# Root per token, padded queries and head pairs, score blocks on ScalarE: one diffusion-backbone step on Trainium2

## The reference

```python
def rms_norm(x, g):
    y = x * lax.rsqrt(jnp.mean(x * x, axis=-1, keepdims=True) + EPS)
    return y * g
def modulated_norm(x, g, mod, j):            # before every sub-layer; scale, shift from c or c_ctx
    return rms_norm(x, g) * (1 + scale) + shift
def half_ffn(x, mod, j, g, w1, w2):
    return x + 0.5 * gate * swiglu(modulated_norm(x, g, mod, j), w1, w2)
# even mixer (8 heads of 64): context tokens attend to context tokens; latent tokens attend to the
# window around them (with a bias table) and to a cached context; beside it a Fourier mix of 4 groups
p = softmax(concat([q @ k_loc.T * scale + bias, q @ ck.T * scale]));  o = p_loc @ v + p_ctx @ cv
# odd mixer (8 heads, state 128x128): gated linear recurrence, forwards and backwards
S = S * exp(b_last) + k_decayed.T @ v;  o = q_decayed @ S + tril(A) @ v
o = rms_norm(o, norm_g) * silu(g)
```

## Time and profile before

| what | value |
|---|---|
| runs | 1718.59, 1720.78, 1723.87 us; median 1720.78 |
| the profiled execution | 1721.95 us, of which the span is 1720.0 us |
| PE busy | 1637.0 us (95%) |
| DVE busy | 1136.2 us (66%) |
| ACT busy | 668.3 us (39%) |
| POOL busy | 148.5 us (9%) |
| chain that ended last | PE 85%, DVE 7%, ACT 3% |
| third norm | residual at 546.1, first product at 553.4 us |

### The profile page before, as it was taken

How to read it: one execution, slowest core, us unless ns; L and a number is a source line. 1 busy time by engine, 2 the same in 40 slices (tenths; PEclk the granted TensorE clock), 3 DMA queues, 4 the chain that set the end, 5 groups by cost and what they waited for, 6 DMA issues and landing times.

```text
span 1720.0 us, 29231 instructions
## 1 busy us (share of the span) xinstructions
PE 1637.0 (95%) x11046; PEld 1560.2 (91%) x11046; DVE 1136.2 (66%) x1962; ACT 668.3 (39%) x881; POOL 148.5 (9%) x196
## 2 busy tenths in 40 slices
PE   4999999889998999999899999989999988999997
PEld 2999999877777999999899999988989878999997
DVE  4788876733346788876788886666767868844334
ACT  3443422422324434322534332255547434444222
POOL 0000000031001000000000000003222000000000
PEclk8999999999999999999999999999999998999999
DMA  9566656764315566555466665644223334544342
GB/s 312 164 183 183 184 160 172 203 191 148 99 50 159 161 188 188 174 167 167 125 186 183 183 177 167 178 160 152 87 89 103 105 99 122 171 124 122 101 135 70
DMA packets 349450, 261.85 MB, mean 152 GB/s; under 512 B 15305, under 2 KB 326978, under 8 KB 349378
## 3 DMA queue, kind: packets, MB, share of 16 engines
q1 hardware_dynamic: 326178, 191.09, 38.5%
q0 software_dynamic: 18432, 67.12, 12.2%
q10 hardware_dynamic: 4768, 2.62, 0.5%
HBM read 257.65 MB, written 3.15 MB: 152 GB/s over the span
## 4 chain that ended last, share of the span: by engine, by line
PE 85%; DVE 7%; ACT 3%; issue 2%; DMA 1%; SPq 1%; POOL 1%; DVEq 0%; POOLq 0%; ACTq 0%
PE bank L1499 24%; PE bank L1501 23%; PE bank L1500 23%; PE bank L1620 2%; DVE w_lo L948 1%; PE bank L1517 1%; SPq L485 1%; DVE rr L1074 1%; PE bank L1785 1%; PE bank L1635 1%; PE bank L1634 1%; ACT w_hi L620 1%; PE bank L1529 1%; PE bank L1625 1%; DMA first_ada<-in_ada_w 1%
## 5 line engine op out<-in xcount | busy, mean ns | idle before, releaser
L948 DVE TENSOR_TENSOR w_lo<-w_raw,w_hi 128x2048 fp32r<-128x2048 f32 (+1 forms) x188 | 390.5, 2077 | 309.6 <-ACT w_hi L620 308.4
L1499 PE MATMUL bank<-xh,w_hi 128*128 128x384 f32 x1568 | 536.2, 342 | 8.3 <-DVE w_lo L948 8.0
L1501 PE MATMUL bank<-xh,w_lo 128*128 128x384 f32 x1568 | 526.6, 336 | 0.0
L1500 PE MATMUL bank<-xl,w_hi 128*128 128x384 f32 x1568 | 526.3, 336 | 0.0
L620 ACT ACTIVATE w_hi<-w_raw 128x2048 fp32r<-128x2048 f32 (+1 forms) x188 | 325.7, 1732 | 267.0 <-PE bank L1501 265.3
L1499 PEld LDWEIGHTS bank<-xh,w_hi 128*128 128x128 f32 x1568 | 295.7, 189 | 16.4 <-issue 10.0
L1500 PEld LDWEIGHTS bank<-xl,w_hi 128*128 128x128 f32 x1568 | 296.0, 189 | 0.4
L1501 PEld LDWEIGHTS bank<-xh,w_lo 128*128 128x128 f32 x1568 | 295.7, 189 | 0.0
L971 DVE SCALAR_TENSOR_TENSOR acc<-ada,cond,acc 128x256 f32<-128x256 f32 x644 | 283.4, 482 | 9.8
L1499 PE MATMUL bank<-gg,w_hi 128*128 128x384 f32 x768 | 258.8, 337 | 0.0
L1501 PE MATMUL bank<-gg,w_lo 128*128 128x384 f32 x768 | 256.7, 334 | 0.0
(11 more groups left out here) (198 smaller groups left out, 1664.0 us busy)
## 6 DMA issues: line engine op xcount, KB each, us to landing
w_raw<-in_ffn_w SPq DMA_DIRECT2D x176, 512.0 KB, 5.0
ada<-in_ada_w POOLq DMA_DIRECT2D x128, 512.0 KB, 4.0
w_raw<-in_mix_w_in SPq DMA_DIRECT2D x56, 512.0 KB, 4.6
w_raw<-in_ffn_w SPq DMA_DIRECT2D x64, 384.0 KB, 3.7
w_raw<-in_ffn_w SPq DMA_DIRECT2D x64, 320.0 KB, 4.1
first_ada<-in_ada_w SPq DMA_DIRECT2D x8, 1024.0 KB, 13.5
w_raw<-in_mix_w_out SPq DMA_DIRECT2D x16, 512.0 KB, 4.5
bias<-in_na_rpb SPq DMA_DIRECT2D x16, 96.0 KB, 6.8
```

The costliest lines, as they stand in the source:

```text
L948: nc.vector.tensor_tensor(w_lo[slot][:, 0:size], w_raw[slot][:, 0:size], w_hi[slot][:, 0:size].bitcast(F32), ALU.subtract).then_inc(s_lo, 1)
L1499: nc.tensor.matmul(out, ah, bh, start=first, stop=False)
L1500: nc.tensor.matmul(out, ah, bl, start=False, stop=False)
L1501: return nc.tensor.matmul(out, al, bh, start=False, stop=last)
```

## The change

1. **Norm.** The mean is made with the squares as stationary operand and two constant columns as moving one, so that token t of a block stands on partition t; root and reciprocal then run over 128x6. `spread`, three matmuls of a broadcast stationary column with the identity, lays the result over all partitions in PSUM (`rb`), where `scaled` reads it. The last square and the first `xh` are cut into the 128 context tokens and the 256 latent ones, each with a wait of its own. In a mixer's norm `spread` stands behind `ada_rows`.
2. **Even mixer.** Queries go into `qz`, 128 partitions for each head with zeros in the other head's half, by four ACT copies of 64 partitions in place of two of 128, after two DVE memsets. Units run in pairs of heads, and `values` takes both heads of a pair at every odd t, alternating between them. `MIX0_ROWS` and `MIX0_BACK` move one block later in chunks 3 to 5. `window` stands behind the second `ada` load.
3. **Odd mixer.** `assemble` becomes part of `far_blocks` on ACT. `next_lo` stands ahead of `start_pair(0)` at i = 3 and ahead of `finish_last(0)` at i = 20. At the end, squares 0 to 3 and their sums run one chunk earlier.

```diff
--- before.py
+++ after.py
-MIX0_ROWS = {2: {1: 1}, 3: {0: 2, 3: 3}, 4: {0: 4, 3: 5}, 5: {0: 6, 3: 7}, 6: {1: 8}, 7: {1: 9}}
-MIX0_BACK = {2: {3: 1}, 3: {2: 2, 5: 3}, 4: {2: 4, 5: 5}, 5: {2: 6, 5: 7}, 6: {3: 8}, 7: {3: 9}}
+MIX0_ROWS = {2: {1: 1}, 3: {0: 2, 4: 3}, 4: {0: 4, 4: 5}, 5: {0: 6, 4: 7}, 6: {1: 8}, 7: {1: 9}}
+MIX0_BACK = {2: {3: 1}, 3: {2: 2, 6: 3}, 4: {2: 4, 6: 5}, 5: {2: 6, 6: 7}, 6: {3: 8}, 7: {3: 9}}
...
-        rr = sb("rr", [P, T])
+        rr = sb("rr", [P, 2 * TB])
...
+        rb = ps[6]
...
-        qT = at("qT", [P, 4, T])
+        qz = at("qz", [P, 2, 4, T])
...
-        units = [(pair, h2, what) for pair in range(4) for h2 in range(2) for what in range(3)]
+        units = [(pair, h2, what) for pair in range(4) for what in range(3) for h2 in range(2)]
...
                 load_pair(pair_at[1] + i + 1, (pair_at[1] + i + 1) // per_layer, 1)
-                if i == 0:
+                if i == 1:
                     pool.wait_ge(s_rpb, 16 * 2 * HEADS)
...
             def squares(m, a, b):
                 for k in range(a, b):
+                    if m and k == KT - 1:
+                        act.wait_ge(s_xg, m)
+                        nc.scalar.activation(xf[:, k, 0:NP_], x[:, k, 0:NP_], ACT.Square)
+                        act.wait_ge(s_x, 8 * m + k + 1)
+                        nc.scalar.activation(xf[:, k, NP_:T], x[:, k, NP_:T], ACT.Square).then_inc(s_sq, 1)
+                        continue
...
-                nc.scalar.activation(rr[:, :], ps[6][:, 0:T], ACT.Sqrt, bias=lb[:, 5, 0:1]).then_inc(s_rs, 1)
+                nc.scalar.activation(rr[:, :], ps[6][:, 0:2 * TB], ACT.Sqrt, bias=lb[:, 5, 0:1]).then_inc(s_rs, 1)
...
-                    act.wait_ge(s_xr, 8 * m + k + 1)
                     for cnd, a, b in GROUPS:
+                        if k == 0 and a == 0:
+                            act.wait_ge(s_xs, m + 1)
+                        else:
+                            act.wait_ge(s_xr, 8 * m + k + 1)
...
+                    elif part == 0:
+                        for h2 in range(2):
+                            rows = slice(HD * h2, HD * h2 + HD)
+                            for e, b in enumerate((b0, b1)):
+                                last = nc.scalar.activation(qz[rows, h2, 2 * half + e, :], b[rows, 0:T], ACT.Copy,
+                                                            scale=HD ** -0.5)
...
                 def far_blocks(pair):
...
+                    act.wait_ge(s_ge, vector_reads[fill_no[pair, "level4"]])
+                    act.wait_ge(s_ga, scalar_reads[fill_no[pair, "far", 1]])
+                    for j in range(COL_GROUPS):
+                        rows = slice(j * BW, (j + 1) * BW)
+                        blocks = amat[rows, :, :].rearrange("p h (c t) -> p (h c) t", t=P)
+                        last = nc.scalar.activation(blocks[:, :, j * BW:(j + 1) * BW], near[rows, :, :], ACT.Copy)
+                    last.then_inc(s_am, 1)
...
                     act.wait_ge(s_used, n0 + 20 + i + 1)
                     next_hi(n0 + 20 + i)
-                squares(s + 1, 0, KT - 1)
+                    if i == 1:
+                        squares(s + 1, 0, 4)
+                squares(s + 1, 4, KT - 1)
...
-                link(nc.vector.reciprocal(rr[:, :], rr[:, :]))
+                nc.vector.reciprocal(rr[:, :], rr[:, :]).then_inc(s_ri, 1)
...
                         last = nc.vector.scalar_tensor_tensor(xf[:, k, a:b], x[:, k, a:b], mod_a[:, k, cnd:cnd + 1],
-                                                              rr[:, a:b], ALU.mult, ALU.mult)
+                                                              rb[:, a:b], ALU.mult, ALU.mult)
...
                 copy_rows(s, 0)
+                for h2 in range(2):
+                    rest = slice(HD * (1 - h2), HD * (1 - h2) + HD)
+                    nc.vector.memset(qz[rest, h2, :, :], 0.0).then_inc(s_qz, 1)
                 next_lo(n0)
...
-                        if task == 6:
-                            assemble(pair)
...
                     if i == 3:
+                        next_lo(n0 + 2)
                         start_pair(0)
                         grow_keys(0, 0)
...
+                    if 3 < i <= 20:
+                        next_lo(n0 + i - 1)
                     if i == 20:
                         finish_last(0)
-                    if 3 <= i <= 20:
-                        next_lo(n0 + i - 1)
-                    if i == 20:
                         finish_last(1)
...
+                    if i == 1:
+                        sum_squares(s + 1, 1, 4)
-                last_residuals(s, n0 + 20, 2)
+                last_residuals(s, n0 + 20, 2, 4)
...
-                    last = nc.tensor.matmul(ps[6][:, 0:T], cst[:, C_MEAN:C_MEAN + P], xf[:, k, :],
-                                            start=(k == 0), stop=(k == KT - 1))
+                    for tb in range(TB):
+                        last = nc.tensor.matmul(rb[:, 2 * tb:2 * tb + 2], xf[:, k, tb * P:(tb + 1) * P],
+                                                cst[:, C_MEAN:C_MEAN + 2], start=(k == 0 and tb == 0),
+                                                stop=(k == KT - 1), skip_group_check=True)
...
+            def spread(m):
+
+                pe.wait_ge(s_ri, m + 1)
+                for tb in range(TB):
+                    last = nc.tensor.matmul(rb[:, tb * P:(tb + 1) * P], rr[:, 2 * tb:2 * tb + 1].broadcast_to([P, P]),
+                                            ident, start=True, stop=True)
+                last.then_inc(s_rb, 1)
...
-                    q = qT[rows, pair, NP_ + b * P:NP_ + (b + 1) * P]
-                    nc.tensor.matmul(scored[:, 0:NS_], q, kT[rows, pair, NP_:T], start=True, stop=False)
+                    q = qz[:, h2, pair, NP_ + b * P:NP_ + (b + 1) * P]
+                    nc.tensor.matmul(scored[:, 0:NS_], q, kT[:, pair, NP_:T], start=True, stop=False)
...
-                    pe.wait_ge(s_pt, u + 1)
-                    out = summed[HD * h2:HD * h2 + HD, what * P:(what + 1) * P]
-                    vals = [vtok[:, 0, cols]] if what == 0 else [vtok[:, 1, cols], vtok[:, 2, cols], cv[:, cols]]
-                    for e, v in enumerate(vals):
-                        last = nc.tensor.matmul(out, v, probT[u % 2][:, e * P:(e + 1) * P],
-                                                start=(e == 0), stop=(e == len(vals) - 1))
-                    last.then_inc(s_pv, 1)
+                    pe.wait_ge(s_pt, u + 2)
+                    blocks = [(vtok, 0)] if what == 0 else [(vtok, 1), (vtok, 2), (cv, None)]
+                    for e, (v, tb) in enumerate(blocks):
+                        for h2 in range(2):
+                            head = 2 * pair + h2
+                            cols = slice(head * HD, head * HD + HD)
+                            last = nc.tensor.matmul(summed[HD * h2:HD * h2 + HD, what * P:(what + 1) * P],
+                                                    v[:, cols] if tb is None else v[:, tb, cols],
+                                                    probT[h2][:, e * P:(e + 1) * P],
+                                                    start=(e == 0), stop=(e == len(blocks) - 1))
...
-                    if t >= 2:
-                        values(t - 2)
+                    if t >= 3 and t % 2:
+                        values(t - 3)
...
                             if MIX0_UNITS[i][k] == 0:
                                 pe.wait_ge(s_ckv, 1)
+                                pe.wait_ge(s_qz, 2)
                                 pe.wait_ge(s_bias, 4)
```

More of the change, by code:

```diff
@@ L283, in build @@
         s_rs = sem("root_ready")
+        s_ri = sem("root_inverted")
+        s_rb = sem("root_spread")
+        s_xg = sem("x_of_prompt_ready")
+        s_xs = sem("x_of_prompt_scaled")
         s_mod = sem("mod_ready")
@@ L709, in copy_chunk @@
                         last = nc.scalar.activation(vtok[:, 2, half * 256:half * 256 + 256], b1[:, 0:256], ACT.Copy)
-                    else:
[L711 to L715, removed]
+                    elif part == 0:
[4 more added lines that the diff above has]
+                                                            scale=HD ** -0.5)
+                    else:
+                        dst = (None, kT, None, fT)[part]
+                        nc.scalar.activation(dst[:, 2 * half, :], b0[:, 0:T], ACT.Copy)
+                        last = nc.scalar.activation(dst[:, 2 * half + 1, :], b1[:, 0:T], ACT.Copy)
                     last.then_inc(s_pj, 1)
@@ L1083, in scaled @@
                         last = nc.vector.scalar_tensor_tensor(xf[:, k, a:b], x[:, k, a:b], mod_a[:, k, cnd:cnd + 1],
-                                                              rr[:, a:b], ALU.mult, ALU.mult)
+                                                              rb[:, a:b], ALU.mult, ALU.mult)
+                        if k == 0 and a == 0:
+                            last.then_inc(s_xs, 1)
                     last.then_inc(s_xr, 1)
@@ L1142, in residual @@
```

(19 more changed lines are left out.)

19 lines of the change are left out of this document (14 added, 5 removed).

## The result

The changed kernel takes 1669.14 us (median of four runs, 1666.3 to 1675.13), the kernel before 1720.4 on the same chips: ratio 0.9704, 95% interval 0.9674 to 0.9735, so 51.3 us less. The profiled execution has a span of 1664.6 us and a time of 1666.3, the lowest of the four; against that of before it is 55.4 us shorter.

The account below looks back on a forecast made before the run. PE bounds the feed-forward stages, so time comes only from norms, PE's own even-mixer instructions and its mixer waits. Norms 15.8, clock 7, even mixer 19.5, odd mixer 11 sum to 53.3 us off 1721.95: 1668, range 1656 to 1688.

Parts of the forecast that it names:

- The norm: Residual to first product 4.8 us in place of 7.2; 15.8 us saved over seven norms; sign: under 5 at each.
- The clock: Behind the norms, PE keeps full clock where five stages began at half clock; 7 us saved, bounds 0 and 10.
- rival (1): Full clock isn't kept behind the norms, mean and `spread` being too little work: 7 us less, 1675; chance 0.14.
- Scores: Even mixer: a long unit's scores take 1.2 us in place of 1.67; 9 us saved in all, bounds 0 and 12.
- Rival (2): Padded queries save nothing, pauses coming from going between fp32 and the products: 9 us less, 1677; chance 0.12.
- Values: Even mixer: values of two heads overlap, about 0.8 us for both; 7.5 us saved, bounds 1.5 and 8.5.
- Rival (3): The two heads' values don't overlap in the even mixer: 6 us less, 1674; chance 0.08.
- Rows, mask, exposed chain: Even mixer: rows save 1.5 us, mask 3 with a 3.4 wait left; 1.5 taken off for less cover on PE.
- Odd mixer: PE's waits for `w_lo` and half clock behind the longest shrink: 11 us saved, 6 to 12; no wait over 1.
- The start: The first norm saves only 0.5 us, being tied to the loads of the first weights.
- (4): A unit's chain (maximum, exponential, scaling, transposes) comes to light in the even mixer, half its gain goes: 1678; chance 0.08.
- (5): Waits in unit after unit put the even mixer at half clock: 75 us of loss, 1743; chance 0.03.

## Why the prediction came out, step by step

The total was right, 1668 against 1669.14, but partly by luck, because errors of opposite sign met: by the marks the norms with the clock gave 6.1 us less than their terms and the odd mixer 1.1 less, the even mixer 7.5 more and the start 1.8 more. One row of the kernel before, the mean of its sixth norm, belongs to the second point:

```profile
1418.16 2.77 PE L1593 MATMUL bank<-xf,cst 128*128 128x384 f32 x4 [2.17 <-DVE xf L1045]
```

- **The norm.** 5.05 us from residual to first product where 4.8 stood; second half of the mean to first product 4.15 in a mixer's norm where it was 5.9. Right, if just over the 5 us named as its sign.
- **The clock.** This step failed: "I expect full clock to be kept, because it fell only in gaps of 3 us and more". It fell with no gap over 1.46 us, at three of five norms, in the sixth behind gaps of at most 0.63. Longest gap was the wrong thing to read from the rows of before. The mean of the sixth norm, of which the prediction says itself that it ran at half clock, came behind a wait of only 2.17 us, as the row above shows. A wait of 2.17 for a `w_lo` in the changed kernel's even mixer left the clock alone. At the third norm PE was busy for 1.76 of 4.00 us between 514 and 518, and with the gaps filled the clock stayed. All norms after the first give 14.0 by the marks (3.8, 29.8 - 27.0, 1.4, 2.4, 14.1 - 12.1, 1.6), where the terms say 20.1 (15.3 less 2.2 for the squares, and 7). So rival (1) was right about the three norms where nothing but mean and `spread` runs; at the mixers' norms `ada_rows` stands between, and that the clock held at both of them was luck in part (it fell at 5 of 20).
- **Scores.** Mechanism right, size off: 1.01 us, not 1.2. The pace taken from the full-height run, 0.24 a record, is 0.22 here, and the two records of 128 columns take 0.14 together where 0.24 stood. 16 x 0.66, 8 x 0.27 for the short ones (0.42 to 0.15) make 12.7 for 9. The way from a transpose to the scores is 0.1 shorter too (0.26 to 0.16 for one, 0.47 to 0.38 for three), 2.3 more for 24 units. Rival (2) is out.
- **Values.** 0.81 for two heads: 7.9 for 7.5. Rival (3) is out. So is, as far as these rows go, the rule of the Trainium skill (TensorE: Matmul & The Clock Gate, Part 3: Packing small matmuls, "What overlaps and what doesn't") that stood behind it: both heads use all 128 rows and overlap, 12 records in 0.81 us where one head's six took 0.80.
- **Rows, mask, exposed chain.** The 3.4 us of wait for the mask is 3.11 in the kernel with the even mixer's edits alone; in the changed kernel it became 2.17 for a `w_lo` ahead and 1.48 for the mask, and the third load is late next (0.55), as said. PE's waits in the stage, without the norm, go from 7.6 to 5.6 us in the kernel with the even mixer's edits alone; the wait for probabilities grew from 0.6 to 1.4, by 0.8 where 1.5 was taken off. Of that kernel's 27.0 us, 12.7 + 2.3 + 7.9 + 2.0 = 24.9 are thus placed; 2.1 stay open. The term was 19.5.
- **Odd mixer.** 12.1 alone, where 11 and 2.2 of the squares stood: right, by the waits named; the longest that is left is 1.2, where none over 1 was expected.
- **The start.** 2.3 us of the profiled 55.4 lie ahead of the first mark, where 0.5 was put down to the first norm. They belong to no edit: with the even mixer's edits alone, which leave the start as it was, they are there too, and with the changed kernel's start they ranged from -2.9 to +3.2 over the runs here.
- **Rivals (4) and (5).** The clock is 1.00 in the even mixer from 374 on, and the exposed chain cost under 1 us.

## What to carry to other kernels

A stretch that waits for a transfer or a long POOL instruction at a fixed time swallows what is won ahead of it; measure parts by marks from stage to stage, since the medians here hide steps of 3 to 5 us that the marks show, and read the clock beside each step, since it alone moved one by 4.8 us. Before a clock is expected to hold in a short chain, ask how much PE does in all of it, and not only how long its longest gap is; idle matmuls there may pay. Give small matmuls the height of their neighbours, by zeros if need be, and put independent ones that fill different columns side by side.

## What was not expected of the hardware

- Two heads' matmuls on different column halves overlap even in program order one after the other: 1.07 us where two heads apart took 1.6.
- 64-row matmuls among 128-row ones took 1.67 us for a set that takes 1.01 with padded rows, more work in less time.
- Behind a wait of 2.17 us the clock was at full in one place and at half in another, and at a mixer's norm the same instructions kept it 15 times of 20.
- The time to the first stage's mark varied by 6 us from one execution to the next, with the same instructions.
